# Differential attention: score products on two 64-row halves at once, three terms each, with the maxima of both maps taken together and the later sums moved back

## The chip, the cores and the metric

The kernel runs on one core of a Trainium2 chip. The core has a matrix engine (PE, with its weight loads shown apart as PEld), a vector engine (DVE), a scalar engine (ACT), GpSimd (POOL) and an engine that issues DMAs (SP). The metric is the device time of one execution in microseconds. Before the change it is 2591.54 us, the median of three runs (2589.82 to 2594.27).

## The reference

One encoder block for 2048 tokens and 16 meta tokens in front of them, D_MODEL = 1024. Four heads of differential attention and four heads of latent attention run side by side, then come an output projection and an MLP. The change touches the differential attention alone. Cut to what it computes:

```python
q1, q2 = q[..., 0, :], q[..., 1, :]      # 4 heads, two maps each, head dimension 64
k1, k2 = k[..., 0, :], k[..., 1, :]
def blk(qp, q1b, q2b):
    mask = _chunk_mask(qp, kpos)          # causal in chunks of 64 keys
    dist = jnp.abs(qp[:, None] - kpos[None, :]).astype(f32)
    bias = jnp.where(mask[None], -slopes[:, None, None] * dist[None], NEG)
    s1 = jnp.einsum('bhqd,bhkd->bhqk', q1b, k1).astype(f32) * scale + bias
    s2 = jnp.einsum('bhqd,bhkd->bhqk', q2b, k2).astype(f32) * scale + bias
    a = jax.nn.softmax(s1, axis=-1) - lam * jax.nn.softmax(s2, axis=-1)
    return jnp.einsum('bhqk,bhkv->bhqv', a.astype(v.dtype), v)   # v: 128 wide
```

## The kernel before, in words

The program is written engine by engine: each stage has one function for each engine, and semaphores join them. The differential attention is the function attention(), between the projections (mla_up) and, behind a barrier of all engines, the latent attention.

Queries and keys come from DRAM as pairs of single-pass numbers, a high part and the small rest (qk_hi, qk_lo). A score is made from these parts. The head dimension is 64 and the engine has 128 rows, so the kernel stacks: the tile of queries (ahead.q, lines 1112 to 1115) holds the high part of one map in rows 0 to 63 and the rest in rows 64 to 127, and the tile of keys holds the high part twice and the rest twice. One matmul over 128 rows then gives two terms, and two matmuls give all four for one map (scores(), matmul at L1613).

A head has 16 rows of work i, each of 128 queries against the 16 + 128 (i + 1) keys that they see. Such a row is cut into chunks of up to 512 keys (row_chunks), for one map c and then for the other. For each chunk:

- PE makes the scores in one of four PSUM banks (da_ps_s, NSB = 4), after DVE has read the chunk that was there (scores_read).
- DVE adds the bias, writes the sum to SBUF (da_rows for the first map, da_second for the other) and keeps the maximum in mx (L1535). After a map's last chunk it takes the maximum over the chunks (L1542).
- ACT takes the exponential of the whole row with its sum (L1481).
- DVE inverts the first map's sum (invert, L1567), POOL scales the first map's row by it (L1473), and DVE inverts the second map's sum (L1574), multiplies that by -lambda (L1576) and adds the second row, so weighted, to the first (end, L1580).

When four rows of a group g are done, PE turns them in tiles of 128 keys (turn, L1646, out to da_ps_t), ACT copies each turned tile into one of NPT = 8 slots of da_pT (L1494), and PE multiplies values by it (product, L1660, out to da_ps_o). A product in full precision shows as two matmul records. The first head also carries twelve products left over from the stage before (late_product, L1629).

All engines walk the same list of steps (STEPS, built by head_steps() from row_steps() and PHASES): chunks in order, with exponentials, scales, ends, turns and products spread between them. PHASES says which groups' turns go under which rows, from which share of them on, and by how many products the products lag behind the turns; SCALE_AFTER and END_AFTER say how many chunks after a row its scale and its end stand. A head's last turns and products go under the next head's rows.

```python
PHASES = (((0, 1), ((1, 3),), 0.2, 7), ((2,), ((0, 0), (0, 1)), 0.15, 7), ((3,), ((0, 2),), 0.2, 7))
SCALE_AFTER, END_AFTER = 2, 5
```

Of the kernel before, what the change touches and what calls it, by code (L numbers as in the profile page):

```python
# [30 lines left out]
P = 128  # L31
# [1075 lines left out]
def by_component(src, h, cols):  # L1107

    return src[ds(h, 1), :, cols].rearrange("a (c p) n -> p (a c) n", c=2)


def load_q(sp, scr, ahead, h, g):
    for j, src in enumerate((scr.qk_hi, scr.qk_lo)):
        sp.dma_start(f32(ahead.q[64 * j:64 * j + 64, g % 2]),
                     by_component(src, h, slice(META + 512 * g, META + 512 * g + 512))).then_inc(ahead.q_loaded[g % 2], 16)


def load_first_keys(sp, scr, ahead, g):

    c0, n = KEY_PIECES[g]  # L1120
    cols = slice(c0, c0 + n)
    for j, src in enumerate((scr.qk_hi, scr.qk_lo)):
        for half in range(2):
            sp.dma_start(f32(ahead.keys[half * 64:half * 64 + 64, j::2, cols]),
                         by_component(src, DA_H, cols)).then_inc(ahead.start_loaded[g], 16)
# [41 lines left out]
def attention(nc, io, scr, ident, ahead, latent):  # L1167
# [8 lines left out]
    with ExitStack() as ctx:  # L1176
        mem = Memory(nc, ctx, io.used)
        keys = (ahead.keys, mem.sb("da_keys", [P, 4, LP], F32R)[:, :, 0:L])
# [5 lines left out]
        NPT = 8  # L1184
        NTB = 3
        pT = mem.sb(f"da_pT", [P, NPT, 512])
        mx = mem.sb("da_mx", [P, 2, COMPS, 5])
        nmax = mem.sb("da_nmax", [P, 2, COMPS])
        nmax_all = mem.sb("da_nmax_all", [P, 5])
        total = mem.sb("da_total", [P, 2, COMPS])  # L1190
        inv = mem.sb("da_inv", [P, 2, COMPS])
        inv2 = mem.sb("da_inv2", [P, 2])
# [15 lines left out]
        inv2_step = mem.sem("da_inv2_step")  # L1208
# [9 lines left out]
        chunks = [(i, c, k0, n) for i in range(NT) for c in range(COMPS) for k0, n in row_chunks(i)]  # L1218
# [4 lines left out]
        KEY_LOADS = 4  # L1223
# [9 lines left out]

        def comp_row(i, c, u):
            return row(i, u) if c == 0 else second[:, i % 2, 0:META + P * (i + 1)]

        def row_steps(carried):
# [4 lines left out]
            for groups, *_ in PHASES:  # L1242
                steps = []
                for n, (i, c, k0, w) in enumerate(chunks):
# [6 lines left out]
                    if k0 + w == META + P * (i + 1):  # L1251

                        steps += [step for _, step in later if step[2] - NT * step[1] < i]
                        later = [(left, step) for left, step in later if step[2] - NT * step[1] >= i]
                        later.append((1, ("exp", 0, i, c)))
                        if c == 0:
                            later.append((SCALE_AFTER, ("scale", 0, i)))
                        if c == COMPS - 1:
                            later.append((END_AFTER, ("end", 0, i)))
# [7 lines left out]
        def cost(step):  # L1267

            if step[0] == "chunk":
                return chunks[step[2]][3] + 60  # L1270
            return META + P * (step[2] + 1) + 250 if step[0] == "end" else 0
# [46 lines left out]
        PHASES = (((0, 1), ((1, 3),), 0.2, 7), ((2,), ((0, 0), (0, 1)), 0.15, 7), ((3,), ((0, 2),), 0.2, 7))  # L1318
        SCALE_AFTER, END_AFTER = 2, 5
# [44 lines left out]
        def _(sp):  # L1364
            def load_keys(h, u):

                for j, src in enumerate((scr.qk_hi, scr.qk_lo)):
                    for half in range(2):
                        sp.dma_start(f32(keys[u][half * 64:half * 64 + 64, j::2, :]),
                                     by_component(src, h + DA_H, slice(0, L))).then_inc(keys_loaded[u], 16)  # L1370
# [95 lines left out]
        def _(pool):  # L1466
# [3 lines left out]
            def scaled(h, i, u, **at):  # L1470

                hold(pool, inv_ready, NT * h + i + 1)
                pool.tensor_scalar(row(i, u), row(i, u), inv[:, i % 2, 0:1], 1.0, ALU.mult, ALU.mult).then_inc(first_scaled, 1)  # L1473
# [4 lines left out]
        def _(act):  # L1478
            def exp(h, i, c, u, **at):
                act.wait_ge(max_ready, NT * COMPS * h + COMPS * i + c + 1)  # L1480
                act.activation(comp_row(i, c, u), comp_row(i, c, u), ACT.Exp, bias=nmax[:, i % 2, c:c + 1], scale=scale,  # L1481
                               accum_out=total[:, i % 2, c:c + 1]).then_inc(exp_ready, 1)
# [5 lines left out]
            def copy(h, g, t, **at):  # L1488
# [5 lines left out]
                act.activation(pT[0:rows_of, n % NPT, c0:512], ps_t[n % NTB][0:rows_of, c0:512], ACT.Copy).then_inc(copied, 1)  # L1494
# [20 lines left out]
        def _(dve):  # L1515
            def chunk(h, n, pair, u):
# [7 lines left out]
                if i % 4 == 0 and c == 0 and k0 == 0:  # L1524
# [4 lines left out]
                    elif g != 1 and not first_head:  # L1529
# [9 lines left out]
                if k0 + w == META + P * (i + 1):  # L1539
# [21 lines left out]
            def invert(h, i, u, **at):  # L1561

                dve.wait_ge(exp_ready, NT * COMPS * h + COMPS * i + 1)
                if not (isinstance(h, int) and h == 0 and i < 2):
# [1924 lines left out]
```

## Time and profile before

| | |
|---|---|
| median of three runs | 2591.54 us |
| the profiled execution | 2589.82 us, its span 2588.0 us |
| PE | 2526.3 us busy, 98% of the span |
| PEld | 2103.8 us, 81% |
| DVE | 1619.0 us, 63% |
| ACT | 1211.9 us, 47% |
| POOL | 333.4 us, 13% |

These shares are averages over stages with different limits. Starts and ends of matmuls are pipelined and the ends are modelled, so the record of a matmul is longer than the time that it holds the engine: the pitch between the starts of matmuls that follow each other tells more. A merged row, such as four matmuls in 0.60 us, runs from the first start to the last end. Idle time that a view puts down to "issue" is time in which the engine waited for nothing that the profile shows.

### The profile page before, as it was taken

The numbers are of one execution on the slowest core, as the hardware profiler recorded it, in microseconds if no ns is written. First come the engines' busy times: TensorE is split into PE (matmuls) and PEld (weight loads), VectorE is DVE, ScalarE is ACT, GpSimd is POOL, SyncE is SP. The second block draws the span as 40 slices with busy tenths as digits, with TensorE's granted clock in tenths as the row PEclk, the third lists the DMA queues.
The fourth block names the chain that finished last, engine by engine and source line by source line (L and its number), as shares of the span: only waits on it lengthen the run. The fifth ranks groups of instructions, "written<-read, shape, count | busy, mean of one in ns | idle before, by whom it ended". The sixth has DMA issues, their size and how long they took to land.

```text
span 2588.0 us, 35257 instructions
## 1 busy us (share of the span) xinstructions
PE 2526.3 (98%) x12140; PEld 2103.8 (81%) x12140; DVE 1619.0 (63%) x3515; ACT 1211.9 (47%) x2183; POOL 333.4 (13%) x368
## 2 busy tenths in 40 slices
PE   8999999999999999989999999999999999999998
PEld 7998887677667989868877888888888888888886
DVE  6123307998995777754468777867757465564765
ACT  6112314777765565554544333533335353443554
POOL 2110002222221222110000000000000001121133
PEclk9999999999999999999999999999999999999999
DMA  6324458553333111145677666666655365776787
GB/s 225 131 100 132 119 164 263 139 136 94 88 134 92 34 30 46 42 130 163 195 240 224 208 221 214 220 193 210 189 165 175 118 216 106 174 166 161 201 165 139
DMA packets 328956, 398.35 MB, mean 154 GB/s; under 512 B 20896, under 2 KB 235184, under 8 KB 320464
## 3 DMA queue, kind: packets, MB, share of 16 engines
q1 hardware_dynamic: 311216, 364.17, 44.8%
q0 software_dynamic: 17568, 31.99, 8.5%
q8 instruction: 95, 1.56, 0.3%
q14 instruction: 77, 0.63, 0.1%
HBM read 239.62 MB, written 156.48 MB: 153 GB/s over the span
## 4 chain that ended last, share of the span: by engine, by line
PE 62%; DVE 3%; DMA 1%; ACT 1%; issue 1%; SPq 0%; POOL 0%; DVEq 0%; ACTq 0%; POOLq 0%
PE ff_ps_x L3277 26%; PE ff_ps_m L3277 13%; PE ff_ps_z L3277 6%; PE ml_ps_s L2153 6%; PE ff_ps_m L1702 4%; PE ml_ps_o L2184 3%; PE ml_ps_t L2166 2%; DMA ml_v_raw<-scr_yT 1%; DMA ff_pieces<-scr_acc 0%; PE ff_ps_r L2714 0%; PE mo_ps_t L2731 0%; SPq L2341 0%; PE ml_ps_o L2180 0%; DVE ff_pieces L2444 0%; DMA work<-scr_w_vo 0%
## 5 line engine op out<-in xcount | busy, mean ns | idle before, releaser
L3277 PE MATMUL ff_ps_x<-ff_mv_hi_p,ff_st_hi_p 128*128 128x512 f32 x764 | 297.8, 390 | 0.5 <-ACT ff_u L3017 0.5
L3277 PE MATMUL ff_ps_x<-ff_mv_lo_p,ff_st_hi_p 128*128 128x512 f32 x764 | 297.3, 389 | 0.0
L3277 PE MATMUL ff_ps_x<-ff_mv_hi_p,ff_st_lo_p 128*128 128x512 f32 x764 | 297.2, 389 | 0.0
L2153 PE MATMUL ml_ps_s<-wide,ml_qs 128*128 128x416 f32 (+14 forms) x880 | 197.0, 358 | 3.0 <-PEq L137 2.8
L3123 DVE TENSOR_TENSOR ff_st_lo_p<-ff_ps_m,ff_st_hi_p 128x512 fp32r<-128x512 f32 x190 | 130.5, 688 | 103.4 <-ACT ff_st_hi_p L3000 103.4
L2967 POOL DMA_DIRECT2D scr_acc<-ff_pieces x64 | 55.5, 872 | 1015.3 <-DVE ff_pieces L3147 946.8
L3017 ACT ACTIVATE ff_u<-ff_ps_x 128x512 f32<-128x512 f32 x128 | 76.6, 598 | 214.9 <-PE ff_ps_x L3277 214.9
L3277 PEld LDWEIGHTS ff_ps_x<-ff_mv_hi_p,ff_st_hi_p 128*128 128x128 f32 x764 | 143.4, 188 | 32.4 <-issue 2.0
L3277 PEld LDWEIGHTS ff_ps_x<-ff_mv_hi_p,ff_st_lo_p 128*128 128x128 f32 x764 | 143.4, 188 | 29.9
L3277 PEld LDWEIGHTS ff_ps_x<-ff_mv_lo_p,ff_st_hi_p 128*128 128x128 f32 x764 | 143.4, 188 | 29.5
L2153 PEld LDWEIGHTS ml_ps_s<-wide,ml_qs 128*128 128x128 f32 x880 | 153.4, 193 | 15.3 <-issue 3.4
L3000 ACT ACTIVATE ff_st_hi_p<-st_raw 128x512 fp32r<-128x512 f32 x191 | 119.4, 626 | 86.3 <-PE ff_ps_z L3277 86.3
L3277 PE MATMUL ff_ps_m<-wide,ff_st_hi_p 128*128 128x512 f32 x512 | 157.7, 389 | 0.4 <-DVE ff_st_lo_p L2618 0.4
L3000 ACT ACTIVATE ff_st_hi_p<-ff_ps_m 128x512 fp32r<-128x512 f32 x190 | 113.2, 598 | 93.7 <-PE ff_ps_m L3277 93.7
L3277 PE MATMUL ff_ps_x<-wide,ff_st_hi_p 128*128 128x512 f32 x504 | 155.1, 389 | 0.0
L3123 DVE TENSOR_TENSOR ff_st_lo_p<-st_raw,ff_st_hi_p 128x512 fp32r<-128x512 f32 x191 | 130.8, 687 | 36.9 <-ACT ff_st_hi_p L3000 35.6
L2062 DVE CUSTOM_DVE_ANT_0 ml_rows<-ml_ps_s,ahead_bias 128x416 f32<-128x416 f32 (+14 forms) x176 | 100.1, 569 | 67.8 <-PE ml_ps_s L2153 59.8
L1660 PE MATMUL da_ps_o<-da_pT,da_v 128*128 128x512 f32 (+3 forms) x320 | 137.2, 529 | 0.0
L1985 ACT ACTIVATE ml_pT_hi<-ml_ps_t 128x512 fp32r<-128x512 f32 (+3 forms) x176 | 90.6, 537 | 88.6 <-PE ml_ps_t L2166 88.5
L1613 PE MATMUL da_ps_s<-da_keys,ahead_q 128*128 128x416 f32 (+14 forms) x352 | 112.6, 423 | 2.4 <-DVE da_mx L1535 2.4
L3277 PEld LDWEIGHTS ff_ps_m<-wide,ff_st_hi_p 128*128 128x128 f32 x512 | 96.0, 188 | 20.5 <-issue 0.6
L3277 PEld LDWEIGHTS ff_ps_x<-wide,ff_st_hi_p 128*128 128x128 f32 x504 | 94.6, 188 | 19.6
(322 smaller groups left out, 6326.1 us busy)
## 6 DMA issues: line engine op xcount, KB each, us to landing
st_raw<-in_w_ff SPq DMA_DIRECT2D x64, 512.0 KB, 6.1
scr_hid<-ff_pieces SPq DMA_DIRECT2D x128, 256.0 KB, 2.7
st_raw<-scr_hid SPq DMA_DIRECT2D x64, 512.0 KB, 5.6
ring<-in_w_ff SPq DMA_DIRECT2D x28, 1024.0 KB, 8.0
scr_t<-ring SPq DMA_DIRECT2D x24, 1024.0 KB, 6.0
ring<-scr_t SPq DMA_DIRECT2D x21, 1024.0 KB, 8.4
scr_acc<-ff_pieces POOLq DMA_DIRECT2D x64, 256.0 KB, 4.1
ring<-scr_u SPq DMA_DIRECT2D x13, 1024.0 KB, 8.0
```

The costliest lines, as they stand in the source:

```text
L1613: m = pe.matmul(ps_s[n % NSB][:, 0:w], qs[:, g % 2, c, P * b:P * b + P], keys[u][:, 2 * c + j, k0:k0 + w], start=j == 0, stop=j == 1)
L1660: pe.matmul(ps_o[:, c0:512], v_meta[:, :] if t == 0 else v[:, t - 1], pT[0:rows_of, n % NPT, c0:512], start=t == 0, stop=t == tiles_of(g) ...
L1702: m = pe.matmul(bank, y[a][:, k], w[b][:, cols], start=k == 0 and i == 0, stop=k == KD - 1 and i == 2, skip_group_check=True)
L1985: act.activation(pT_hi[0:rows_of, n % NPT, c0:512], ps_t[n % NTB][0:rows_of, c0:512], ACT.Copy).then_inc(hi_copied, 1)
L2062: dve.tensor_tensor_reduce(out=row(i, u)[:, k0:k0 + w], in0=ps_s[n % NSB][:, 0:w], in1=bias[:, b0:b0 + w], scale=1.0, scalar=LOWEST, op0=A ...
L2153: m = pe.matmul(ps_s[n % NSB][:, 0:w], q, k, start=j == 0, stop=j == len(pairs) - 1)
L2184: m = pe.matmul(ps_o[:, c0:512], v[0:rows_of, t - 1], p, start=False, stop=t == tiles_of(g) - 1 and j == 2)
L2967: pool.dma_start(piece_place(scr.acc, name, n), piece[name][u], accum_op=ALU.add).then_inc(added[name][u], 16)
L3000: act.activation(st_hi[kind][:, :, :], stationary(kind, n % 2), ACT.Copy).then_inc(st_hi_ready, 1)
L3017: act.activation(tile, bank[:, :], ACT.Copy).then_inc(taken, 1)
L3123: dve.tensor_tensor(st_lo[kind][:, :, :], stationary(kind, n % 2), f32(st_hi[kind][:, :, :]), ALU.subtract).then_inc(st_lo_ready, 1)
L3277: m = pe.matmul(bank[:, :], w[kind][:, k], a[kind][:, k], start=start and k == 0 and i == 0, stop=stop and k == KH - 1 and i == 2, skip_gr ...
```

## The change

Queries and keys are laid out by map instead of by part: rows 0 to 63 hold the first map, rows 64 to 127 the second, and high part and rest lie side by side along the columns. A chunk of keys is now worked on for both maps in turn: the list of chunks goes map by map within each chunk. On PE, at the first map's chunk, six matmuls of 64 rows each are issued: for each of three terms (high by high, high by rest, rest by high; the term rest by rest is gone) one on rows 0 to 63 into one bank and one on rows 64 to 127 into the next. They wait for both banks of the pair.

On DVE the bias step multiplies by -scale and keeps a minimum, and one reduction (most, L1546) makes both maps' values for the exponentials, one chunk after the row's end; both exponentials follow it. The second map's inversion, its weight and the sum are separate steps now (invert, weigh, end), placed by row_end() further behind. Their small tiles have eight slots, the second map's rows have three places (da_third), and the turned tiles twelve. PHASES starts turns later and lets products lag by eleven.

```diff
 def load_q(sp, scr, ahead, h, g):
     for j, src in enumerate((scr.qk_hi, scr.qk_lo)):
-        sp.dma_start(f32(ahead.q[64 * j:64 * j + 64, g % 2]),
-                     by_component(src, h, slice(META + 512 * g, META + 512 * g + 512))).then_inc(ahead.q_loaded[g % 2], 16)
+        sp.dma_start(f32(ahead.q[:, g % 2, j]),
+                     flat(src[ds(h, 1), :, META + 512 * g:META + 512 * g + 512])).then_inc(ahead.q_loaded[g % 2], 16)
...
-        chunks = [(i, c, k0, n) for i in range(NT) for c in range(COMPS) for k0, n in row_chunks(i)]
+        chunks = [(i, c, k0, n) for i in range(NT) for k0, n in row_chunks(i) for c in range(COMPS)]
...
+        def row_end(i):
+            n = len(row_chunks(i))
+            scale, invert = {NT - 1: (5, 10), 0: (4, 10), 1: (4, 9), 2: (4, 8)}.get(i) or (n + 2, 2 * n + 2)
+            return (("most", 1), ("exp", 1, 0), ("exp", 1, 1), ("scale", scale),
+                    ("invert", invert), ("weigh", invert + 1), ("end", invert + 2))
...
-        PHASES = (((0, 1), ((1, 3),), 0.2, 7), ((2,), ((0, 0), (0, 1)), 0.15, 7), ((3,), ((0, 2),), 0.2, 7))
-        SCALE_AFTER, END_AFTER = 2, 5
+        PHASES = (((0, 1), ((1, 3),), 0.35, 11), ((2,), ((0, 0), (0, 1)), 0.2, 11), ((3,), ((0, 2),), 0.3, 11))
...
             def load_keys(h, u):
                 for j, src in enumerate((scr.qk_hi, scr.qk_lo)):
-                    for half in range(2):
-                        sp.dma_start(f32(keys[u][half * 64:half * 64 + 64, j::2, :]),
-                                     by_component(src, h + DA_H, slice(0, L))).then_inc(keys_loaded[u], 16)
+                    sp.dma_start(f32(keys[u][:, j, :]), flat(src[ds(h + DA_H, 1), :, 0:L])).then_inc(keys_loaded[u], 16)
...
                 dve.tensor_tensor_reduce(out=comp_row(i, c, u)[:, k0:k0 + w], in0=ps_s[n % NSB][:, 0:w],
-                                         in1=bias[u][:, b0:b0 + w], scale=1.0, scalar=LOWEST,
-                                         op0=ALU.add, op1=ALU.max,
-                                         accum_out=mx[:, i % 2, c, nth:nth + 1]).then_inc(scores_read, 1)
-                if k0 + w == META + P * (i + 1):
-                    dve.wait_ge(scores_read, NCH * h + n + 1)
-                    dve.tensor_scalar(nmax_all[:, 0:nth + 1], mx[:, i % 2, c, 0:nth + 1], -scale, None, ALU.mult, ALU.min,
-                                      accum_out=nmax[:, i % 2, c:c + 1]).then_inc(max_ready, 1)
+                                         in1=bias[u][:, b0:b0 + w], scale=-scale, scalar=-LOWEST,
+                                         op0=ALU.add, op1=ALU.min,
+                                         accum_out=mx[:, i % 4, c, nth:nth + 1]).then_inc(scores_read, 1)
...
+            def most(h, i, **at):
+                last = max(n for n, chunk in enumerate(chunks) if chunk[0] == i)
+                dve.wait_ge(scores_read, NCH * h + last + 1)
+                dve.tensor_reduce(nmax[:, i % NR8, :], mx[:, i % 4, :, 0:len(row_chunks(i))], AX.X, ALU.min).then_inc(max_ready, 1)
...
-                if not (isinstance(h, int) and h == 0 and n < NSB):
-                    pe.wait_ge(scores_read, NCH * h + n - NSB + 1)
-                for j in range(2):
-                    m = pe.matmul(ps_s[n % NSB][:, 0:w], qs[:, g % 2, c, P * b:P * b + P], keys[u][:, 2 * c + j, k0:k0 + w],
-                                  start=j == 0, stop=j == 1)
-                m.then_inc(scores_ready, 1)
+                if c == 0:
+                    if not (isinstance(h, int) and h == 0 and n + 1 < NSB):
+                        pe.wait_ge(scores_read, NCH * h + n + 1 - NSB + 1)
+                    for j, (of_q, of_k) in enumerate(((0, 0), (0, 1), (1, 0))):
+                        for comp in range(COMPS):
+                            half = slice(64 * comp, 64 * comp + 64)
+                            m = pe.matmul(ps_s[(n + comp) % NSB][:, 0:w], qs[half, g % 2, of_q, P * b:P * b + P],
+                                          keys[u][half, of_k, k0:k0 + w], start=j == 0, stop=j == 2)
+                            if j == 2:
+                                m.then_inc(scores_ready, 1)
```

The instructions of PE in the second head, at rows 7 and 8 of work, before (each line one line of the program, da_ps_s the scores, da_ps_t the turned tiles, da_ps_o the value products):

```order
L1613 MATMUL da_ps_s<-da_keys,ahead_q 128x352 x2
L1613 MATMUL da_ps_s<-da_keys,ahead_q 128x336 x2
L1646 MATMUL da_ps_t<-ident,da_rows 128x128 x5
L1660 MATMUL da_ps_o<-da_pT,da_v 128x512
L1613 MATMUL da_ps_s<-da_keys,ahead_q 128x352 x2
L1646 MATMUL da_ps_t<-ident,da_rows 128x128
L1613 MATMUL da_ps_s<-da_keys,ahead_q 128x352 x2
L1660 MATMUL da_ps_o<-da_pT,da_v 128x512
L1613 MATMUL da_ps_s<-da_keys,ahead_q 128x336 x2
L1613 MATMUL da_ps_s<-da_keys,ahead_q 128x416 x2
L1660 MATMUL da_ps_o<-da_pT,da_v 128x512
```

The same engine and place in the change:

```order
L1620 MATMUL da_ps_s<-da_keys,ahead_q 128x352 x6
L1654 MATMUL da_ps_t<-ident,da_rows 128x128 x7
L1620 MATMUL da_ps_s<-da_keys,ahead_q 128x352 x6
L1668 MATMUL da_ps_o<-da_pT_more,da_v 128x512
L1654 MATMUL da_ps_t<-ident,da_rows 128x128 x3
L1620 MATMUL da_ps_s<-da_keys,ahead_q 128x336 x6
L1668 MATMUL da_ps_o<-da_pT_more,da_v 128x512
L1620 MATMUL da_ps_s<-da_keys,ahead_q 128x416 x6
```

Chunks of two matmuls have become pairs of six, with turns and value products on both sides of nearly each pair. Within one such six, in the first head (the number behind da_ps_s is the bank):

```order
L1620 MATMUL da_ps_s2<-wide,ahead_q 128x352
L1620 MATMUL da_ps_s3<-wide,ahead_q 128x352
L1620 MATMUL da_ps_s2<-wide,ahead_q 128x352
L1620 MATMUL da_ps_s3<-wide,ahead_q 128x352
L1620 MATMUL da_ps_s2<-wide,ahead_q 128x352
L1620 MATMUL da_ps_s3<-wide,ahead_q 128x352
```

The two maps, and with them the two halves of the rows, alternate. On DVE, in the first head around the sum of row 7 (128x1040), before:

```order
L1535 ISA da_rows,da_mx<-da_ps_s,ahead_bias 128x336
L1535 ISA da_mx 128x1
L1542 TENSOR_SCALAR da_nmax_all,da_nmax<-da_mx 128x3
L1574 RECIPROCAL da_inv<-da_total 128x1
L1576 TENSOR_SCALAR da_inv<-da_inv,da_lam 128x1
L1580 SCALAR_TENSOR_TENSOR da_rows<-da_second,da_inv,da_rows 128x1040
```

And in the change:

```order
L1546 TENSOR_REDUCE da_nmax<-da_mx 128x2
L1536 ISA da_second,da_mx<-da_ps_s,ahead_bias 128x448
L1536 ISA da_mx 128x1
L1572 RECIPROCAL da_inv<-da_total 128x1
L1536 ISA da_rows,da_mx<-da_ps_s,ahead_bias 128x448
L1536 ISA da_mx 128x1
L1578 TENSOR_SCALAR da_inv<-da_inv,da_lam 128x1
L1536 ISA da_second,da_mx<-da_ps_s,ahead_bias 128x448
L1536 ISA da_mx 128x1
L1584 SCALAR_TENSOR_TENSOR da_rows<-da_second,da_inv,da_rows 128x1040
```

The four small steps that stood in a row now have chunks between them, and one reduction serves both maps.

## Rows read from the trace of the kernel before

**Rows 1.** Stages: us, PE, PEld, DVE, ACT, POOL busy (instructions), clock, DMA share, GB/s

```profile
506.30:592.70 86.40, 83.45 (x417) 61.37 (x417) 78.38 (x305) 63.16 (x112) 19.01 (x16) 1.00 0.47 111
592.70:679.00 86.30, 83.36 (x417) 61.42 (x416) 78.25 (x305) 63.27 (x112) 19.02 (x16) 1.00 0.46 111
679.00:765.30 86.30, 83.38 (x417) 61.41 (x417) 78.25 (x304) 63.20 (x112) 19.03 (x16) 1.00 0.33 111
```

**Rows 2.** Chain of waits: start us, us, what

```profile
1389.14 2.72 PE ff_ps_z L3277 x12
```

**Rows 3.** Timeline of PE at L721, 128-row transposes: start us, us, engine, line, operation

```profile
225.07 0.36 PE L707 MATMUL cv_ps<-cv_w_hi,u_lo 128*128 128x448 f32 x1
225.27 0.60 PE L721 MATMUL cv_pt<-ident,o_hi 128*128 128x128 f32 x4
...
225.91 0.37 PE L707 MATMUL cv_ps<-w_lo,u_hi 128*128 128x448 f32 x1
```

**Rows 4.** PE by line, 425 to 800 us: instructions xcount | busy us, mean ns | idle

```profile
L1660 PE MATMUL da_ps_o<-da_pT,da_v 128*128 128x512 f32 (+3 forms) x320 | 137.2, 529 | 0.0
L1613 PE MATMUL da_ps_s<-da_keys,ahead_q 128*128 128x416 f32 (+14 forms) x352 | 112.6, 423 | 2.4 <-DVE da_mx L1535 2.4
L1613 PE MATMUL da_ps_s<-wide,ahead_q 128*128 128x416 f32 (+14 forms) x352 | 105.1, 407 | 3.8 <-DVE da_mx L1535 3.7
L1646 PE MATMUL da_ps_t<-ident,da_rows 128*128 128x128 f32 x608 | 90.3, 273 | 6.5 <-DVE da_rows L1580 6.5
L1660 PE MATMUL da_ps_o<-da_pT,da_v_meta 128*128 128x512 f32 x32 | 16.7, 605 | 1.4 <-ACT da_pT L1494 1.4
```

**Rows 5.** Timeline of PE after the last scores

```profile
775.09 1.02 PE L1660 MATMUL da_ps_o<-da_pT,da_v 128*128 128x512 f32 x2
775.95 0.60 PE L1646 MATMUL da_ps_t<-ident,da_rows 128*128 128x128 f32 x4
...
795.52 4.68 PE L2153 MATMUL ml_ps_s<-wide,ml_qs 128*128 128x144 f32 x17 [2.76 <-PEq L137]
```

**Rows 6.** Waits of PE, 506.3 to 765.3: us in total, times, longest

```profile
PE da_ps_t L1646 <- DVE da_rows L1580: 3.8, 3, 1.3
PE da_ps_s L1613 <- DVE da_mx L1535: 3.6, 6, 0.8
```

**Rows 7.** Longest wait of DVE, the same stretch

```profile
DVE da_rows L1535 <- PE da_ps_s L1613: 5.4, 12, 0.6
```

**Rows 8.** Timeline of the weight loads, the same place

```profile
219.96 0.32 PEld L721 LDWEIGHTS cv_pt<-ident,o_hi 16*128 16x128 f32 x4 [0.31 <-issue]
220.31 0.19 PEld L707 LDWEIGHTS cv_ps<-w_hi,u_hi 128*128 128x128 f32 x1
220.41 0.19 PEld L707 LDWEIGHTS cv_ps<-w_lo,u_hi 128*128 128x128 f32 x1
```

**Rows 9.** Timeline of PE around the 16-row transposes

```profile
219.66 0.37 PE L707 MATMUL cv_ps<-cv_w_hi,u_lo 128*128 128x448 f32 x1
219.96 0.42 PE L721 MATMUL cv_pt<-ident,o_hi 16*128 16x16 f32 x4
220.31 0.47 PE L707 MATMUL cv_ps<-w_hi,u_hi 128*128 128x448 f32 x1
220.62 0.36 PE L707 MATMUL cv_ps<-w_lo,u_hi 128*128 128x448 f32 x1
```

**Rows 10.** Timeline of PE where products of 16 output columns end

```profile
305.70 0.39 PE L707 MATMUL cv_ps<-cv_w_hi,u_lo 128*16 128x512 f32 x1
305.93 0.60 PE L721 MATMUL cv_pt<-ident,o_hi 128*128 128x128 f32 x4
```

**Rows 11.** Timeline of DVE at the end of a row of work

```profile
627.46 0.08 DVE L1535 DVE_READ_ACCUMULATOR2_ANT da_mx<- 128x1 f32 x1
...
627.66 0.16 DVE L1574 RECIPROCAL da_inv<-da_total 128x1 f32<-128x1 f32 x1
...
628.10 1.30 DVE L1580 SCALAR_TENSOR_TENSOR da_rows<-da_second,da_inv,da_rows 128x1040 f32<-128x1040 f32 x1
```

More of the change, by code:

```diff
@@ L1122, in load_first_keys @@
     for j, src in enumerate((scr.qk_hi, scr.qk_lo)):
-        for half in range(2):
-            sp.dma_start(f32(ahead.keys[half * 64:half * 64 + 64, j::2, cols]),
-                         by_component(src, DA_H, cols)).then_inc(ahead.start_loaded[g], 16)
+        sp.dma_start(f32(ahead.keys[:, j, cols]), src[DA_H, :, cols]).then_inc(ahead.start_loaded[g], 16)
 def load_first_head(sp, io, scr, ahead, g):
@@ L1177, in attention @@
         mem = Memory(nc, ctx, io.used)
-        keys = (ahead.keys, mem.sb("da_keys", [P, 4, LP], F32R)[:, :, 0:L])
+        NPT, NPT_MORE = 12, 4
+        keys = (ahead.keys, mem.sb("da_keys", [P, 2, LP], F32R)[:, :, 0:L])
+        third = mem.sb("da_third", [P, LP])
+        pT_more = mem.sb("da_pT_more", [P, NPT_MORE, 512])
+        mem.sb("da_keys_place", [P, LP - NPT_MORE * 512])
         qs = ahead.q
@@ L1232, in row, with pT_of @@
             return rows[u ^ (g == 2)][:, i % 4, start:start + META + P * (i + 1)]
+        def pT_of(n):
+            n %= NPT
+            return pT[:, n] if n < NPT - NPT_MORE else pT_more[:, n - NPT + NPT_MORE]
         def comp_row(i, c, u):
-            return row(i, u) if c == 0 else second[:, i % 2, 0:META + P * (i + 1)]
+            if c == 0:
+                return row(i, u)
+            at, start = (1, sum(META + P * (a + 1) for a in range(i))) if i < 5 else (i % 3, 0)
+            return (third if at == 2 else second[:, at])[:, start:start + META + P * (i + 1)]
         def row_steps(carried):
@@ L1250, in row_steps @@
                     later = [(left, step) for left, step in later if left > 0]
-                    if k0 + w == META + P * (i + 1):
[L1253 to L1259, printed above, removed]
+                    if c == COMPS - 1 and k0 + w == META + P * (i + 1):
+                        later += [(left, (kind, 0, i, *at)) for kind, left, *at in row_end(i)]
                 phases.append(steps)
             return phases, [(left, (step[0], 1) + step[2:]) for left, step in later]
+        def row_end(i):
[3 more added lines that the diff above has]
+                    ("invert", invert), ("weigh", invert + 1), ("end", invert + 2))
         def first_chunk(i):
@@ L1270, in cost @@
                 return chunks[step[2]][3] + 60
-            return META + P * (step[2] + 1) + 250 if step[0] == "end" else 0
+            return META + P * (step[2] + 1) + 100 if step[0] == "end" else 0
         def head_steps():
@@ L1559, in minus_lambda, with invert_first @@
                 dve.wait_ge(lam_step, 4)
-            def invert(h, i, u, **at):
+            def invert_first(h, i, u, **at):
                 dve.wait_ge(exp_ready, NT * COMPS * h + COMPS * i + 1)
-                if not (isinstance(h, int) and h == 0 and i < 2):
-                    dve.wait_ge(first_scaled, NT * h + i - 1)
-                dve.reciprocal(inv[:, i % 2, 0:1], total[:, i % 2, 0:1]).then_inc(inv_ready, 1)
-            def end(h, i, u, **at):
+                if not (isinstance(h, int) and h == 0 and i < NR8):
+                    dve.wait_ge(first_scaled, NT * h + i - NR8 + 1)
+                dve.reciprocal(inv[:, i % NR8, 0:1], total[:, i % NR8, 0:1]).then_inc(inv_ready, 1)
@@ L1578, in end @@
                 dve.wait_ge(first_scaled, NT * h + i + 1)
-                dve.scalar_tensor_tensor(out=row(i, u), in0=comp_row(i, 1, u), scalar=inv2[:, i % 2:i % 2 + 1], in1=row(i, u),
+                dve.scalar_tensor_tensor(out=row(i, u), in0=comp_row(i, 1, u), scalar=inv2[:, i % NR8:i % NR8 + 1], in1=row(i, u),
                                          op0=ALU.mult, op1=ALU.add).then_inc(probs_ready, 1)
-            heads(dve, {"chunk": chunk, "scale": invert, "end": end})
+            heads(dve, {"chunk": chunk, "most": most, "scale": invert_first, "invert": invert_second, "weigh": weigh_second, "end": end})
```

50 lines of the change are left out of this document (24 added, 26 removed).

## The prediction, made before the changed kernel ran

> **What bounds the kernel now.** I read the stage table first. Of the four heads of the differential attention the three later ones take 86.4, 86.3 and 86.3 us, and in the middle one PE is busy 83.36 us, DVE 78.25, ACT 63.27, POOL 19.02, all at a granted clock of 1.00, the 2.4 GHz level [rows 1]. The reader is to see that two engines are nearly full, so the next question is how much of PE's busy time is work. The chain of waits gives the pitch of a single-pass product: twelve of 512 columns in 2.72 us, 0.227 us each [rows 2]; one of 448 columns takes 0.20 us (225.07 to 225.27) [rows 3]. On the line through the two, 401 columns, the mean width of a score chunk (17,664 columns in 44 chunks by row_chunks), take 0.18 us. A head has 176 score matmuls (704 in the two groups of L1613 over four heads), 152 transposes (608) and 88 records of value products, two to each of 44 products [rows 4]. A product of 512 columns takes 0.86 us (775.09 to 775.95) [rows 5]; four transposes take 0.60 us with 0.27 us for the last, so one each 0.11 us [rows 3, 4]. Per head: scores 176 x 0.18 = 31.7 us; values 19,456 columns = 38 x 512, 38 x 0.86 = 32.7; transposes 152 x 0.11 = 16.7; together 81 of 86.3 us. So PE is the bound, with about 5 us of slack, and its waits agree: in 259 us of three heads it stood 3.8 us for finished rows and 3.6 us for score banks, both from DVE [rows 6], while DVE's longest wait for PE sums to 5.4 us [rows 7]. The latent attention starts at 795.52 us, behind a barrier, and PE stood 2.76 us before it [rows 5]; nothing later overlaps this stage, so what it gains or loses passes to the end one for one.
>
> **The change part by part.** *Products.* A pair of chunks (both maps, same keys) costs 4 x 0.18 = 0.72 us on 128 rows now; it becomes six matmuls of 64 rows. If the two halves run side by side, that is 3 x 0.18 = 0.54 us, if one after the other 6 x 0.18 = 1.08. There are 44 pairs a head, 176 in all: -32 us at the one end, +63 at the other. In between lies the weight path: two weight loads that nothing hides start 0.10 to 0.11 us apart (220.31, 220.41) [rows 8], and six in a row would take 0.63 us, -16 us in all. No row shows two halves at once. I take -32, since the shape asks for it (each half has its own rows and its own bank) and the loads of 16 rows stand closer, four in 0.42 us with their matmuls [rows 9], so loads need not be the limit.
>
> The Trainium skill (TensorE: Matmul & The Clock Gate, Part 3: Packing small matmuls) says that matmuls on different row groups run together with some 4 ns for each further tile; by it the six would cost about 0.55 us and the term -30. No run here shows it.
>
> *Switches.* The new rows of the engine's order show six half-height matmuls, then transposes or value products on all 128 rows, then six again. Over the stage the score matmuls stand in 170 separate runs, almost one to each of the 176 pairs. The trace has one such excursion, the 16-row transposes of L721: from the last full product (219.66) through four transposes to the second full product (220.62) 0.96 us pass [rows 9]. The same place with 128-row transposes takes 0.84 us (225.07 to 225.91) [rows 3]. But the four small transposes need little themselves: their records span 0.42 us, the last about 0.21 of it, so 0.07 each at most, 0.06 by their weight loads, where the tall ones take 0.11. Without a price for the change 0.84 - 0.43 + 0.25 = 0.66 us would do; the excursion costs 0.30 us. It isn't a wait: the first small weight load has 0.31 us of idle before it, put down to issue [rows 8], and the next tall load starts only at 220.31, after the small ones are through. On the other side, a change from 16 columns of output to 128 costs nothing: 305.70, 305.93, 0.23 us apart, as 512 columns are [rows 10]. So the bounds are 0 and 0.38 us (0.30 plus a first load of single-pass weights, 0.10 for the 0.02 seen with 16 rows). I take 0.30, the row nearest in kind, rows against rows: 170 x 0.30 = +51 us; the ends are 0 and +65.
>
> The Trainium skill (TensorEngine Tiling (Array Packing), Key Properties) has it that changing the tiling mode drains the engine, a rule against this change. The trace agrees for rows with 0.30 us and doesn't for columns with nothing; a column change that cost as much as a row change would leave the sum as it is.
>
> *Maxima and sums.* DVE loses 32 small reductions a head and gets 16. One now stands between the accumulator read that ends at 627.54 and the next instruction at 627.66, 0.12 us; the inversion and weighing behind it hold DVE until 628.10 [rows 11]. One reduction fewer in a row, and no standing between inverse, weight and sum, is 0.15 to 0.3 us for each of 16 rows, 2.5 to 5 us a head. With PE the bound that is worth only PE's waits for DVE, 7.4 us in three heads [rows 6], about 10 in four. I take half, -5 us; the ends are 0 and -10. The exponentials of both maps now run one after the other on ACT, up to 4 us without a copy from the transpose banks; ACT has 23 us free a head [rows 1], and the later sums and twelve instead of eight slots for turned tiles lie in front of it: nothing, with 2 us a head as the upper end.
>
> *Loads.* The keys of a head are no longer stored twice, half the bytes in two issues instead of four; queries go in two as before. Neither engine stood for a load in these three heads [rows 6, 7], so nothing. SP's order is kept, and nothing new is queued behind a wait there. The new waits on PE are the same in kind: a pair waits for the banks of the pair before last, where a chunk waited for the fourth last.
>
> Sum: -32 + 51 - 5 = +14 us. The profiled execution took 2589.8 us (span 2588.0); that is 1.7 under the median of 2591.5. From it: 2604 us.
>
> **The rivals.** (1) Half-height matmuls join the stream like the 16-column products do, without a price. Then PE drops to 81 - 8 = 73 us a head and DVE, at 78 less 2.5 to 5, is level with it. With PE's 5 us of slack kept the head takes 78 us, four heads save 32: 2558. For it speaks the column change of [rows 10]; against it the one change in rows there is. (2) The price is there but about half, 0.15 us, because 64 rows leave the array sooner into tall work or the next load hides behind the other half: -32 + 26 - 5 = -11, 2579. (3) Weight loads for both halves go one by one and the first stands open: -16 + 65 - 5 = +44, 2634. For it, loads 0.10 us apart; against it, the small ones. (4) The halves don't run together, so the change doesn't do what it says: +63 + 51 - 5 = +109, 2699. Nothing in the trace excludes it. The other side of my forecast is rivals 1 and 2, and the point that decides is the price of one excursion: below (32 + 5) / 170 = 0.22 us the kernel gets faster.
>
> **How the numbers follow.** Forecast (price 0.25 to 0.38, halves together) 0.42; rival 1 0.20; rival 2 0.20; rival 3 0.12; rival 4 0.06. A measurement of this kernel tells about 0.2%, 5 us, from no change. Rival 2's upper edge and the forecast's lower edge lie within that: 0.05 and 0.06. So faster 0.20 + 0.15 = 0.35, same 0.11, slower 0.36 + 0.12 + 0.06 = 0.54. The forecast's own range is 2594 to 2622. For eight in ten both signs are needed: from 2556, rival 1 with little to spare, to 2636, which holds rival 3 and leaves out rival 4.
>
> **What the changed profile would show.** Right: the second half's matmul starts within a few hundredths of a microsecond of the first, a six spans about 0.55 us, and between a run of score matmuls and the tall work on either side PE's starts are some 0.1 to 0.2 us later than the pitch, with the weight load behind the gap put down to issue; heads of about 90 us; DVE's busy share down to some 82%. Wrong in the price: tall weight loads already issued while half-height matmuls run, heads under 84 us. Wrong in the products: halves starting 0.18 us apart (rival 4) or loads 0.1 us apart with matmuls waiting for them (rival 3). If ACT's copies turn up as what PE's transposes wait for, the two exponentials in a row weren't free.

## The result, and the profile after

The changed kernel takes 2677.18 us (median of 4 runs, 2671.11 to 2682.32) against 2590.68 us: ratio 1.0332, 95% interval [1.0305, 1.0359]. The forecast's side was right (slower), its size was not: +86 us, where it said +14, and 2677 lies outside the range of 2556 to 2636. The profiled run's span is 2669.3 us at a mean granted clock of 0.987, and the loss is in the stage named: the latent attention starts at 878.09 us, 82.57 us later than before [rows 5].

Stages of the profile after, in the columns of [rows 1], which they answer:

```profile
521.40:628.60 107.20, 93.90 (x508) 53.85 (x506) 72.41 (x256) 61.85 (x112) 18.93 (x17) 0.95 0.20 70
628.60:736.80 108.20, 94.90 (x506) 53.71 (x504) 72.55 (x256) 61.67 (x112) 18.87 (x17) 0.94 0.20 69
736.80:845.90 109.10, 95.78 (x506) 54.70 (x504) 72.54 (x256) 61.88 (x112) 18.81 (x17) 0.92 0.25 88
```

A head takes 108 us instead of 86. DVE lost 5.8 us of work a head (72.5 for 78.3), a little over the 2.5 to 5 that the forecast gave the small reductions. But PE's busy time grew, and nothing is full any more: on PE 13 us a head are idle. Its waits in the profile after, 521.4 to 845.9 us (us in total, times, longest), answer [rows 6]:

```profile
PE da_ps_t L1654 <- DVE da_rows L1584: 17.1, 6, 2.9
PE da_ps_o L1668 <- ACT o_out L1502: 14.6, 3, 4.9
PE da_ps_t L1654 <- ACT da_pT_more L1495: 8.2, 6, 1.6
```

39.9 us in three heads, where the kernel before has 8.8: 7.4 in [rows 6] and 1.4 for ACT's copies [rows 4]. And DVE, whose longest wait for scores summed to 5.4 us [rows 7], now has this line for the same stretch:

```profile
DVE da_rows L1536 <- PE da_ps_s L1620: 103.3, 83, 7.1
```

PE waits for DVE and ACT, and DVE waits for PE: they take turns.

First the part that went as forecast. The profile after, timeline of PE around one pair of chunks (start us, us, engine, line, operation), as in [rows 9]:

```profile
648.15 0.94 PE L1654 MATMUL da_ps_t<-ident,da_rows 128*128 128x128 f32 x7
649.02 0.84 PE L1620 MATMUL da_ps_s<-wide,ahead_q 64*128 64x416 f32 x6
649.79 1.12 PE L1668 MATMUL da_ps_o<-da_pT,da_v 128*128 128x512 f32 x2
```

and the weight loads of the same place, as in [rows 8]:

```profile
648.28 0.58 PEld L1654 LDWEIGHTS da_ps_t<-ident,da_rows 128*128 128x128 f32 x5
649.02 0.49 PEld L1620 LDWEIGHTS da_ps_s<-wide,ahead_q 64*128 64x128 f32 x6 [0.17 <-issue]
649.79 0.30 PEld L1668 LDWEIGHTS da_ps_o<-da_pT,da_v 128*128 128x128 f32 x2 [0.28 <-issue]
```

The first two of the six by themselves (PEld in the window 649.00 to 649.03, PE in 649.00 to 649.10):

```profile
649.02 0.19 PEld L1620 LDWEIGHTS da_ps_s<-wide,ahead_q 64*128 64x128 f32 x2 [0.17 <-issue]
649.02 0.46 PE L1620 MATMUL da_ps_s<-wide,ahead_q 64*128 64x416 f32 x2
```

Two loads together take the 0.19 us of one [rows 8], and the two matmuls have started before 649.10. Six matmuls of 416 columns go in 0.77 us from the first start to the next work's, where six in a row at 0.18 us would need 1.1: the halves run side by side, loads and all. And the first load on either side of the pair stands open behind 0.17 and 0.28 us of idle that is put down to issue, to no engine. That is where the excursion shows (the change from 128-row work to half height and back); what it costs, the runs below measure.

Now the new part. The last sum of a group of rows on DVE, in the timeline of DVE in the profile after, behind the last chunk that PE had made:

```profile
640.50 0.15 DVE L1546 TENSOR_REDUCE da_nmax<-da_mx 128x2 f32<-128x4 f32 x1
...
641.00 2.37 DVE L1584 SCALAR_TENSOR_TENSOR da_rows<-da_second,da_inv,da_rows 128x2064 f32<-128x2064 f32 x1
```

and PE at that time:

```profile
639.71 0.92 PE L1668 MATMUL da_ps_o<-da_pT,da_v 128*128 128x256 f32 x4
643.42 1.59 PE L1654 MATMUL da_ps_t<-ident,da_rows 128*128 128x128 f32 x12 [2.80 <-DVE da_rows L1584]
644.83 1.22 PE L1668 MATMUL da_ps_o<-da_pT,da_v_meta 128*128 128x512 f32 x1
```

The reader is to see that the transposes of 643.42 stand in PE's order right behind a sum that itself stands late in DVE's. The same at ACT: its timeline in the profile after, where PE's next product waits for the copy to o_out,

```profile
695.46 1.59 ACT L1482 ACTIVATE da_rows<-da_rows,da_nmax 128x1552 f32<-128x1552 f32 x1 [2.39 <-DVE da_nmax L1546]
...
697.05 1.57 ACT L1482 ACTIVATE da_third<-da_third,da_nmax 128x1552 f32<-128x1552 f32 x1
...
698.62 0.57 ACT L1502 ACTIVATE o_out<-da_ps_o 128x512 f32<-128x512 f32 x1
```

and PE:

```profile
693.60 0.87 PE L1620 MATMUL da_ps_s<-wide,ahead_q 64*128 64x448 f32 x6
699.34 1.19 PE L1668 MATMUL da_ps_o<-da_pT,da_v_meta 128*128 128x512 f32 x1 [4.87 <-ACT o_out L1502]
```

Such a stop costs twice. Stages of the profile after, in the columns of [rows 1], around the first of these two and then around the second:

```profile
640.50:643.40 2.90, 0.13 (x2) 0.00 (x0) 2.90 (x6) 2.02 (x5) 0.00 (x0) 1.00 0.17 66
643.42:644.83 1.41, 1.41 (x13) 1.30 (x13) 0.02 (x1) 0.66 (x2) 0.00 (x0) 0.97 0.49 186
644.83:647.50 2.67, 2.67 (x8) 1.17 (x8) 0.00 (x0) 0.92 (x2) 0.00 (x0) 0.50 0.00 0
695.00:699.30 4.30, 0.00 (x0) 0.00 (x0) 2.58 (x7) 3.73 (x5) 0.00 (x0) 0.61 0.26 91
699.30:702.50 3.20, 3.16 (x4) 1.17 (x4) 0.00 (x0) 0.00 (x0) 0.00 (x0) 0.50 0.22 82
```

At the first, PE stood for 2.8 us, ran transposes at a granted clock of 0.97, and then had 2.67 us at 0.50, the 1.2 GHz level. At the second, the clock fell while PE stood (0.61), and the 3.2 us of products behind the stop ran at 0.50.

### The profile page after: what moved, and what is told of

Read it like the earlier page. It is cut to its first block, busy times and chain, and to the rows that moved or that the text cites. A ratio compares the mean times of both kernels' runs of the same rounds, so it can differ in the third digit from the quotient of the medians.

```text
span 2669.3 us, 35745 instructions
## 1 busy us (share of the span) xinstructions
PE 2566.8 (96%) x12492; PEld 2069.5 (78%) x12492; DVE 1596.9 (60%) x3323; ACT 1206.0 (45%) x2183; POOL 333.5 (12%) x368
## 4 chain that ended last, share of the span: by engine, by line
PE 60%; DVE 3%; DMA 1%; ACT 1%; issue 1%; POOL 0%; SPq 0%; DVEq 0%; ACTq 0%; POOLq 0%
PE ff_ps_x L3285 25%; PE ff_ps_m L3285 12%; PE ff_ps_z L3285 6%; PE ml_ps_s L2161 6%; PE ff_ps_m L1710 4%; PE ml_ps_o L2192 3%; PE ml_ps_t L2174 2%; DMA ml_v_raw<-scr_yT 1%; DMA ff_pieces<-scr_acc 0%; PE ff_ps_r L2722 0%; PE mo_ps_t L2739 0%; PE ml_ps_o L2188 0%; DVE ff_pieces L2452 0%; DVE ff_pieces L2643 0%; DVE ff_pieces L2639 0%
## 5 line engine op out<-in xcount | busy, mean ns | idle before, releaser
L1654 PEld LDWEIGHTS da_ps_t<-ident,da_rows 128*128 128x128 f32 x608 | 71.2, 146 | 72.7 <-issue 26.4
L1654 PE MATMUL da_ps_t<-ident,da_rows 128*128 128x128 f32 x608 | 95.3, 290 | 32.1 <-DVE da_rows L1584 21.1
L1482 ACT ACTIVATE da_rows<-da_rows,da_nmax 128x144 f32<-128x144 f32 (+7 forms) x64 | 77.6, 1213 | 106.8 <-DVE da_nmax L1546 106.8
L1474 POOL TENSOR_SCALAR da_rows<-da_rows,da_inv 128x144 f32<-128x144 f32 (+7 forms) x64 | 75.8, 1187 | 350.5 <-DVE da_inv L1568 350.5
```

Of the source, the lines that this page charges most:

```text
L1474: pool.tensor_scalar(row(i, u), row(i, u), inv[:, i % NR8, 0:1], 1.0, ALU.mult, ALU.mult).then_inc(first_scaled, 1)
L1654: m = pe.transpose(ps_t[n % NTB][0:rows_of, P * b:P * b + P], row(4 * g + b, u)[:, k0:k0 + rows_of], ident[:, :])
```

## The experiments

Two theories at first. **Switches:** the price of an excursion was set too low. **Order:** the new places of the row's end cost PE stalls that the forecast did not have. In the runs called "tall" the pair's products have 128 rows, four in all, so that no excursion is left; those called "half" keep the half-height products. Ratios are to the kernel before.

**a1_tall.**

```diff
-for j, (of_q, of_k) in enumerate(((0, 0), (0, 1), (1, 0))):
-    for comp in range(COMPS):
-        m = pe.matmul(..., qs[half, g % 2, of_q, ...], keys[u][half, of_k, k0:k0 + w], ...)
+for comp in range(COMPS):
+    for j in range(2):
+        m = pe.matmul(..., qs[:, g % 2, 0, ...], keys[u][:, j, k0:k0 + w], ...)
```

> The changed kernel with each pair's six half-height matmuls replaced by four of 128 rows (the maps' scores are summed over both, so the values differ; the amount of work is that of the kernel before). No switch of height is left, the new order and the later sums stay. If the switches are the root of the loss: PE's work is 81 us a head again, the waits for finished rows and output copies shrink with it, 2580 to 2600 us. If the new order and the later sums lose the time by themselves (PE standing some 13 us a head): 2630 us or more.

2637.34 us, 1.0182 [1.0165, 1.0199] of before, 97 to 99 us a head. The longest waits of PE and of DVE in its trace, 518.8 to 813.1 us:

```profile
PE da_ps_t L1652 <- DVE da_rows L1584: 16.0, 6, 2.7
PE da_ps_o L1666 <- ACT o_out L1502: 13.5, 3, 4.6
DVE da_rows L1536 <- PE da_ps_s L1619: 77.1, 68, 5.9
```

Without a single half-height matmul 47 us of the 86 are lost, by the same waits as in the changed kernel. The order theory has more than half of the loss; the products and switches have 40.

**a2_two_terms.**

```diff
-((0, 0), (0, 1), (1, 0))
+((0, 0), (0, 1))
```

> The changed kernel with two terms instead of three: the third (rest of the query by high key) is left out, two half-height matmuls fewer in each of 176 pairs, the same 170 runs and switches. If PE's stream is what counts: 176 x 0.18 = 32 us less than the change, about 2645. If heads are set by waits in the step order, with PE standing anyway: less than 15 us less, above 2662.

2665.1 us, 1.0286 [1.0266, 1.0307]. A term of 176 pairs by 0.18 us would be 32 us; only 12 came. The whole stage from the first score to the latent attention, in the columns of [rows 1], in the changed kernel and then in a2_two_terms:

```profile
426.70:878.10 451.40, 394.83 (x2090) 229.05 (x2089) 295.77 (x1039) 254.40 (x462) 76.00 (x65) 0.94 0.24 85
428.30:869.90 441.60, 380.95 (x1738) 206.56 (x1737) 294.37 (x1039) 255.28 (x463) 75.95 (x65) 0.89 0.25 87
```

PE is idle for 57 us of the stage in the one and for 61 in the other, and the mean clock is 0.94 and 0.89. An estimate from these: a clock of 0.94 costs 0.06 x 451 = 27 us, one of 0.89 costs 0.11 x 442 = 49. So what is missing of the 32 us, 20, is about what the lower clock took back. The work left PE's stream; the stops, and the clock behind them, stayed.

**b1_small_half and b1_small_tall** measure the price by itself, in the kernel before.

```diff
+pe.matmul(ps_s[n % NSB][:, 0:64], qs[0:64, g % 2, c, P * b:P * b + P], keys[u][0:64, 2 * c, k0:k0 + 64], ...)   # half
+pe.matmul(ps_s[n % NSB][:, 0:64], qs[:, g % 2, c, P * b:P * b + P], keys[u][:, 2 * c, k0:k0 + 64], ...)         # tall
```

> The kernel before with one more small matmul ahead of each of 352 chunks, 64 rows by 64 columns, into the bank that the chunk overwrites. That is 352 changes to half height and back. If one costs 0.37 us as read in the changed kernel's trace: +130 us less some 15 of slack, 2700 to 2725. If half height has no price of its own: like the twin with 128 rows, 2600 to 2620.

> The twin of the run with small half-height matmuls: the same 352 small matmuls of 64 columns, over 128 rows. No change of height. Each costs a weight load's 0.11 us at most: 352 x 0.11 = 39 us, less up to 16 us of slack: 2600 to 2630. By no theory as much as the half-height twin if the switch has a price.

Half height 2719.29 us (1.0495 [1.0474, 1.0516]), tall 2618.74 us (1.0107 [1.0087, 1.0127]): 100.5 us for 352 excursions, 0.286 us each, against the forecast's 0.30. PE's timeline of the half-height one:

```profile
601.90 0.60 PE L1648 MATMUL da_ps_t<-ident,da_rows 128*128 128x128 f32 x4
602.42 0.29 PE L1612 MATMUL da_ps_s<-da_keys,ahead_q 64*128 64x64 f32 x1
602.65 0.70 PE L1615 MATMUL da_ps_s<-da_keys,ahead_q 128*128 128x480 f32 x2
```

From the small matmul to the next tall one it is 0.23 us; in the tall twin, at the place shown, it is 0.04 us (599.91 to 599.95):

```profile
599.91 0.19 PE L1612 MATMUL da_ps_s<-da_keys,ahead_q 128*128 128x64 f32 x1
599.95 0.62 PE L1615 MATMUL da_ps_s<-da_keys,ahead_q 128*128 128x416 f32 x2
```

So the question was what in the order costs 47 us. **Placement:** only PE's waiting steps stand too close behind what they wait for. **Dependency:** rows and banks come late, and wherever PE's step stands the wait turns up.

**c1_tall_turns, c2_tall_outs, c3_tall_all, c4_half_all.** A pass over the list of steps keeps transposes, value products and copies out in their order, but holds a group's first transposes behind its last sum, or its first product behind the copy out, and the second exponential behind the first (in chunk steps; a pair of chunks is two). The pass itself, spread(), is left out here.

```diff
-STEPS = head_steps()
+STEPS = spread(head_steps(), turn_gap=5, out_gap=0, exp_gap=0)   # c1
+STEPS = spread(head_steps(), turn_gap=0, out_gap=5, exp_gap=0)   # c2
+STEPS = spread(head_steps(), turn_gap=5, out_gap=5, exp_gap=2)   # c3, and c4 on the changed kernel
```

> The kernel with four full-height products to a pair (values differ), and PE's first transposes of a group moved five chunk steps behind the row sum they need. Placement theory: the 16.0 us in three heads that PE stood for finished rows go, some 5 us a head, so about 2637 - 20 = 2617 us, and the wait of the first transposes for DVE's row end falls under 4 us in three heads. Dependency theory (PE is late because rows and banks come late, wherever its steps stand): the wait turns up elsewhere, 2630 to 2640.

> The same full-height kernel, with only the first product of a group moved five chunk steps behind ACT's copy of the group before. Placement theory: the 13.5 us in three heads that PE stood for that copy go, some 4.5 us a head, so about 2619 us. Dependency theory: 2630 to 2640, with the wait at another of PE's places.

> The full-height kernel with both moves, and the second map's exponential two chunk steps behind the first's on ACT. Placement theory: the three waits (16.0, 13.5, 8.3 us in three heads) go, 12.6 us a head, so 2637 - 45 = 2592, 2585 to 2605; that is the time of the kernel before. Dependency theory: 2620 to 2640.

> The changed kernel, half-height products and all, with the three moves. Placement theory: 39.9 us of waits in three heads go, 13.3 a head, so 2677 - 53 = 2624, and up to 15 less if the clock no longer falls behind the stalls: 2605 to 2630; heads of 92 to 94 us. Dependency theory: 2660 or more.

| run | us | ratio |
|---|---|---|
| c1_tall_turns | 2665.26 | 1.0292 [1.0274, 1.0309] |
| c2_tall_outs | 2633.34 | 1.0167 [1.015, 1.0183] |
| c3_tall_all | 2631.01 | 1.016 [1.0143, 1.0177] |
| c4_half_all | 2670.63 | 1.0312 [1.0294, 1.0329] |

My placement theory fell: c2_tall_outs and c3_tall_all gain 4 and 6 us on a1_tall, c4_half_all gains 7 on the changed kernel, and c1_tall_turns lies above the range of either theory. In c1_tall_turns the wait for the sum is gone, and PE (522.5 to 840.9 us) stands for other things, 28 us worse than a1_tall:

```profile
PE da_ps_o L1704 <- ACT o_out L1540: 13.5, 3, 4.6
PE da_ps_s L1657 <- DVE da_mx L1574: 13.5, 9, 2.3
PE da_ps_t L1690 <- ACT da_pT L1533: 11.3, 6, 3.4
```

What is held back has less room left, and bunches. So the cause lies in front of PE's steps: either the sums stand too late, or the chain of both maps together is too long wherever they stand.

**d1 to d4.** By row_end() the sum that closes a group stands 8, 10, 12 and 12 chunk steps behind its row's last chunk, in the order of the four groups (the expectation of d1_tall_ends has 12 to 14); in the kernel before, where the next map's end forces it out, it is 1 to 4. The edit puts all sums at 9: those of the last two groups three steps sooner, that of the first one step later. A phase is a part of the head's rows under which PHASES puts the transposes and products of finished groups; its start is the share of those rows that goes by first.

```diff
-scale, invert = {NT - 1: (5, 10), 0: (4, 10), 1: (4, 9), 2: (4, 8)}.get(i) or (n + 2, 2 * n + 2)
-return (("most", 1), ("exp", 1, 0), ("exp", 1, 1), ("scale", scale), ("invert", invert), ("weigh", invert + 1), ("end", invert + 2))
+return (("most", 1), ("exp", 1, 0), ("exp", 2, 1), ("scale", 5), ("invert", 8), ("weigh", 9), ("end", 9))   # d1, d2, d3
-PHASES = (..., 0.35, 11), (..., 0.2, 11), (..., 0.3, 11)
+PHASES = (..., 0.35, 9), (..., 0.35, 11), (..., 0.35, 7)   # d2, d3
+PHASES = (..., 0.2, 7), (..., 0.15, 7), (..., 0.2, 7)      # d4, with row_end() as changed
```

> The kernel with four full-height products to a pair (values differ), and the end of a row sooner: the second exponential 2 chunk steps behind the row, the sum at 9 instead of up to 14. Late-sums theory (sums 12 to 14 chunk steps behind their row push transposes and value products together, and PE and DVE then stand for each other in turn): two thirds or more of the 47 us that this kernel with the given order lost come back, 2595 to 2610, heads of 88 to 91 us. Both-maps theory (with the maxima of both maps together the chain to the sum is too long wherever the sum stands): 2625 to 2640.

> The same, with the starts of the three phases at 0.35 (and 9, 11, 7 products put off). Late-sums theory: 2585 to 2600, the time of the kernel before, with heads of 85 to 88 us and PE's waits below 3 us a head. Both-maps theory: 2620 to 2640.

> The changed kernel with half-height products, with the sooner row ends and the starts of the run before this one. Late-sums theory: the order's 47 us go and what stays is products -32 and excursions at 0.29 to 0.37 us, +50 to +65: 2605 to 2625, heads of 91 to 95 us. If the halves could profit once the order is mended: below 2590. Both-maps theory: 2650 or more.

> The full-height kernel with the late sums as they are, and only the phases' starts and put-off products as in the kernel before (0.2, 0.15, 0.2; 7). Late-sums theory: transposes come earlier but stand for rows that aren't summed yet, so only a part comes back, 2610 to 2630, with PE's waits for finished rows above 16 us in three heads. Rival (the late starts alone push the work together): 2590 to 2605.

| run | us | ratio |
|---|---|---|
| d1_tall_ends | 2603.3 | 1.0046 [1.003, 1.0063] |
| d2_tall_ends_starts | 2601.22 | 1.0035 [1.0022, 1.0047] |
| d3_half_ends_starts | 2625.57 | 1.0128 [1.0111, 1.0145] |
| d4_tall_starts | 2623.47 | 1.0124 [1.0107, 1.014] |

Row ends at 9 give 34 of the 47 us back. The starts and lags of the kernel before, alone, give 14 (d4); later starts, together with the row ends, 2 more (d2). Both d2_tall_ends_starts and d3_half_ends_starts end 1 us above the range expected. The row ends were not run together with the starts of the kernel before. DVE's wait for scores in d1_tall_ends, 507.4 to 777 us, has fallen from the 77.1 us of a1_tall:

```profile
DVE da_rows L1534 <- PE da_ps_s L1617: 47.8, 60, 2.8
```

d4_tall_starts shows why early starts alone don't do: transposes come sooner, for rows that are not summed (509.3 to 795 us):

```profile
PE da_ps_t L1652 <- DVE da_rows L1584: 20.4, 6, 3.6
```

With the order mended, half-height products still cost 24 us: d3_half_ends_starts less d2_tall_ends_starts, same steps. Its heads take 93 to 95 us.

**e1 to e4** part what d1 moved together, and undo the pairs.

```diff
-("most", 1), ("exp", 1, 0), ("exp", 1, 1), ("scale", scale), ("invert", invert), ("weigh", invert + 1), ("end", invert + 2)
+("most", 1), ("exp", 1, 0), ("exp", 2, 1), ("scale", scale), ...                                   # e1
+("most", 1), ("exp", 1, 0), ("exp", 1, 1), ("scale", 5), ("invert", 8), ("weigh", 9), ("end", 9)   # e2, and e4 on the changed kernel
-chunks = [... for k0, n in row_chunks(i) for c in range(COMPS)]
+chunks = [... for c in range(COMPS) for k0, n in row_chunks(i)]         # e3, and a wait for one bank at a time
```

> The full-height kernel in the given order (values differ), with one step moved: the second exponential 2 instead of 1 chunk steps behind the row; the sums stay late. Late-sums theory: at most a fourth of the 34 us comes back, 2628 to 2638. Rival, two exponentials in a row (they keep ACT from PE's copies): most of it comes back, 2603 to 2615.

> The full-height kernel in the given order, with the exponentials in a row as they were and only the sums sooner: scaling at 5, inversion at 8, weight and sum at 9 chunk steps. Late-sums theory: 2600 to 2610, the 34 us again. Rival, two exponentials in a row: 2628 to 2638.

> The full-height kernel with the late sums, its chunks again map by map as in the kernel before and a wait for each single bank; maxima of both maps still together. Late-sums theory: nothing comes back, 2632 to 2650. Rival, chunks in pairs (two banks at a time leave PE and DVE less room): 2600 to 2615.

> The changed kernel with half-height products, and only the sums sooner, as in the run of the sums alone. Late-sums theory: 2625 to 2640, some 40 to 50 us below the changed kernel. Rival, two exponentials in a row: 2665 to 2680.

| run | us | ratio |
|---|---|---|
| e1_tall_exp | 2633.26 | 1.0169 [1.0152, 1.0186] |
| e2_tall_sums | 2606.57 | 1.0057 [1.004, 1.0074] |
| e3_tall_by_map | 2648.35 | 1.0223 [1.0206, 1.024] |
| e4_half_sums | 2634.11 | 1.0165 [1.0148, 1.0182] |

Moving the second exponential is worth 4 us, the pairs nothing (without them it is 11 us worse). The sums, with the scaling, inversion and weighing in front of them, give back 31 us in the tall kernel and 43 in the changed one. PE's waits in e2_tall_sums over the stage, 427.6 to 811.8 us:

```profile
PE da_ps_s L1617 <- DVE da_mx L1534: 9.3, 13, 1.6
PE da_ps_t L1650 <- ACT da_pT_more L1493: 6.9, 8, 1.1
PE da_ps_t L1650 <- DVE da_rows L1582: 6.3, 5, 1.8
```

Over the same stage of a1_tall PE stands 19.6 us for finished rows and 18.1 for the copy out; here the first is down to 6.3 (6.5 in the kernel before) and the second is gone. DVE still waits 57.8 us for scores, against 96.6 in a1_tall and 6.2 before. A middle head of e4_half_sums, columns as in [rows 1]:

```profile
613.60:710.90 97.30, 90.26 (x506) 51.92 (x508) 74.91 (x263) 61.53 (x113) 18.98 (x16) 1.00 0.22 78
```

11 us less than the same head of the changed kernel, of which PE's busy time is 4.6, with the clock back at 1.00 (0.97 in the heads on either side). No version ran faster than the kernel before.

## Why the prediction was right and wrong

**Products, -32: held, as far as rows show it.** The halves and their loads run side by side. Six matmuls of 416 columns take 0.77 us; less the 0.19 that half height adds on the way out (0.23 for 0.04, the b1 rows), that is 0.58, close to the prediction's three pitches, 0.54, and far from six, 1.08. No run measured the term by itself; with 0.58 it would be -25, an estimate. Rival 4 fell, and of rival 3 the loads one by one; its open first load is there. The Trainium skill (TensorE: Matmul & The Clock Gate, Part 3: Packing small matmuls) has further row groups run along at some 4 ns each; an estimate by it is three pitches and little more for the six. The trace agrees, by the same 0.77 us, way out included.

**Switches, +51: held.** By themselves 0.286 us an excursion; in the mended order 24 us net, which with -32 is +56, 0.32 us for each of 176 pairs, and with -25 is +49, 0.28 us each. Rivals 1 and 2 needed at most 0.15. So the point that decided, 0.22 us, was the right question, and the row chosen, the 16-row transposes, the right row. The side, slower, came out by this mechanism and not by luck: with the order mended the half-height kernel is still slower than its tall twin. The Trainium skill (TensorEngine Tiling (Array Packing), Key Properties) has a change of tiling mode drain the engine, without a figure. For rows the runs agree, with 0.28 to 0.32 us there and back.

**Maxima and sums, -5: the step that failed.** It counted what the edit takes off DVE, and of the row end's new places it priced only ACT's exponentials ("nothing, with 2 us a head as the upper end"). On the chip everything in the edit but the half-height products is +47 (a1_tall), with 34 of it in where the row ends stand, 31 of that in the sums and the steps just in front of them. The upper end covered ACT, whose share was 4 us, and not the sums themselves: row_end() in the diff puts them 8 to 12 chunk steps behind their row, and the prediction took the later sums as cover ("lie in front of it") where they were the price. What it said of PE's new waits ("the same in kind") was said of the score banks, and there it held: PE's waits for banks are not among the three of the profile after. The waits that grew it left out: [rows 6] had 3.8 us for finished rows in three heads, the profile after 17.1, and 14.6 for a copy that no row of before shows it standing for. Its own sign for ACT, copies that PE's transposes wait for, did turn up (8.2 us); e1_tall_exp shows that it pointed at 4 us only.

**What is left:** -32 + 56 + 47 = +71 of +86. The other 15 or so appear only with both, half-height products in the late order (40 us there, 24 in the mended one). The whole stage, in the columns of [rows 1], in the kernel before, a1_tall, d2_tall_ends_starts and d3_half_ends_starts:

```profile
427.20:795.50 368.30, 351.36 (x1737) 259.22 (x1736) 318.66 (x1232) 260.40 (x463) 77.29 (x67) 1.00 0.47 125
428.30:844.40 416.10, 362.83 (x1738) 269.18 (x1736) 293.87 (x1039) 254.15 (x463) 76.16 (x65) 0.96 0.27 92
426.50:806.30 379.80, 356.91 (x1737) 266.27 (x1735) 299.03 (x1039) 254.29 (x462) 76.50 (x65) 0.98 0.29 101
430.00:832.50 402.50, 381.53 (x2089) 222.13 (x2089) 300.77 (x1039) 254.61 (x463) 76.44 (x65) 0.99 0.28 95
```

By the estimate made for a2_two_terms the clock costs some 27 us in the changed kernel and 17 in a1_tall, 10 more with half height; in the mended order it costs 4 with half height and 8 without. That is 14 of the 15; no run held the clock fixed, so it remains an estimate. The same rows part the 47 of a1_tall: PE is idle 53 us of the stage instead of 17, and the clock costs some 17, together a little more than the whole. It was not settled what keeps the mended tall order 10 us behind the kernel before.

**The mechanism,** as far as shown: when a group's last sum comes late, its transposes and value products are confined to what is left of the phase; PE then first stands, and later has all its tall work at once, while DVE starves. Shown are the alternating waits, that moving PE's steps only moves the wait (c1), and that moving the sums brings PE's wait for finished rows back to that of the kernel before and 31 of the 47 us with it (e2), and 43 of the 86 in the changed kernel (e4). With the sums, the first transposes of the last two groups, which stand right behind them, came one or two steps sooner too; no run moved the sums and left the transposes where they were. That it is the room left in the phase, rather than some single distance, is my reading.

## What to carry to other kernels

When a change re-places steps in a hand-made order on engines that are 90% full, price the places before the instructions: count for each producer how many steps it stands behind its data, and what must still fit in behind it. Giving the late step's consumers more distance gained 7 us at best here and lost 28 at worst; bringing the producers forward gained 31 to 43. And a packing gain is to be set against the number of times that the stream enters and leaves it: 0.18 us gained and 0.3 paid per pair was lost from the start.

## What was not expected of the hardware

The low clock can come behind a stop of PE rather than in it: after the stop of 2.80 us the transposes right behind it ran at 0.97, and the 2.67 us after them at 0.50 (rows above). Taking work off PE bought less than the work here: a2_two_terms has a third of the score products less, and its stage a clock of 0.89 instead of 0.94. Two half-height weight loads with different rows start together: two take 0.19 us and six 0.49, where two tall ones in a row start 0.10 us apart [rows 8].
